# The hand-written order of weight splits against attention steps in the mixing layers of a two-block network, moved by a tile or a unit

## The reference

```python
def second_block(x, ...):
    for i in range(2):
        x = x + 0.5 * _swiglu(_rmsnorm(x, ffn1_norm[i]), ...)      # 1024 -> 2 x 2816 -> 1024
        x = x + _mixing(_rmsnorm(x, mix_norm[i]), ...)             # the layer that is changed
        x = x + 0.5 * _swiglu(_rmsnorm(x, ffn2_norm[i]), ...)
    return _rmsnorm(x, final_norm)
```

## Time and profile before

| What | Value |
|---|---|
| Median of 3 runs (lowest, highest) | 1243.99 us (1242.6, 1244.24) |
| Profiled execution: its time, its span | 1242.6 us, 1240.8 us |
| Mean granted TensorE clock | 0.997 |
| Busy in the span: PE, DVE, ACT, POOL | 99%, 70%, 55%, 13% |
| TensorE's weight loads busy | 94% |
| HBM read, mean rate | 218.48 MB, 177 GB/s |

### The profile page before, as it was taken

The page is one execution under the profiler, slowest core; times in us unless marked ns, Lnnn a source line. Parts: engine busy times, 40 slices in busy tenths (PEclk is TensorE's granted clock), DMA queues, the critical chain, the costliest instruction groups (busy, mean ns, idle before and its releaser), DMA issues.

```text
span 1240.8 us, 24135 instructions
## 1 busy us (share of the span) xinstructions
PE 1229.7 (99%) x10072; PEld 1160.3 (94%) x10072; DVE 869.3 (70%) x1372; ACT 684.7 (55%) x1100; POOL 160.2 (13%) x210
## 2 busy tenths in 40 slices
PE   9999999999999999999999999999999999999997
PEld 7889878999999988899999999999998889999997
DVE  6988798878665557867666556677556777766742
ACT  7674666555545466556554544555447566555541
POOL 4201500275000110012000010000120002000001
PEclk9999999999999999999999999999999999999998
DMA  9545643556565554345555555655555444655550
GB/s 328 183 120 176 240 138 127 178 181 211 191 200 187 188 185 138 119 137 193 199 190 201 188 187 204 201 185 186 194 186 171 137 134 139 204 203 183 191 188 35
DMA packets 61388, 221.09 MB, mean 178 GB/s; under 512 B 7264, under 2 KB 7392, under 8 KB 61024
## 3 DMA queue, kind: packets, MB, share of 16 engines
q1 hardware_dynamic: 60768, 218.87, 53.4%
q0 software_dynamic: 224, 0.53, 0.2%
q10 hardware_dynamic: 288, 0.16, 0.0%
HBM read 218.48 MB, written 1.05 MB: 177 GB/s over the span
## 4 chain that ended last, share of the span: by engine, by line
PE 94%; DVE 4%; ACT 1%; issue 1%; POOL 1%; DMA 0%; POOLq 0%; ACTq 0%; DVEq 0%
PE pb L476 13%; PE pb L478 13%; PE pb L477 13%; PE pb L491 8%; PE pb L493 8%; PE pb L492 8%; PE pb L456 7%; PE pb L458 7%; PE pb L457 7%; PE pb L549 3%; DVE s_acc L1388 2%; PE pb L578 1%; DVE s_wl L1236 1%; PE pb L602 1%; PE pb L736 1%
## 5 line engine op out<-in xcount | busy, mean ns | idle before, releaser
L1236 DVE TENSOR_TENSOR s_wl<-s_wraw,s_wh 128x1024 fp32r<-128x1024 f32 (+1 forms) x411 | 501.7, 1241 | 125.9 <-ACT s_wh L877 125.4
L877 ACT ACTIVATE s_wh<-s_wraw 128x1024 fp32r<-128x1024 f32 (+1 forms) x411 | 420.8, 1048 | 181.1 <-PE pb L478 83.0
L476 PE MATMUL pb<-s_xh,s_wh 128*128 128x256 f32 x1296 | 359.1, 277 | 0.0
L478 PE MATMUL pb<-s_xh,s_wl 128*128 128x256 f32 x1296 | 358.3, 276 | 0.0
L477 PE MATMUL pb<-s_xl,s_wh 128*128 128x256 f32 x1296 | 358.3, 276 | 0.0
L477 PEld LDWEIGHTS pb<-s_xl,s_wh 128*128 128x128 f32 x1296 | 243.5, 188 | 0.0
L476 PEld LDWEIGHTS pb<-s_xh,s_wh 128*128 128x128 f32 x1296 | 243.5, 188 | 0.0
L478 PEld LDWEIGHTS pb<-s_xh,s_wl 128*128 128x128 f32 x1296 | 243.4, 188 | 0.0
L456 PE MATMUL pb<-s_wh,s_xh 128*128 128x512 f32 x448 | 180.9, 404 | 1.6 <-DVE s_wl L1236 1.6
L491 PE MATMUL pb<-s_hh,s_wh 128*128 128x256 f32 x660 | 182.2, 276 | 0.0
L492 PE MATMUL pb<-s_hl,s_wh 128*128 128x256 f32 x660 | 182.2, 276 | 0.0
(11 more groups left out here) (313 smaller groups left out, 1590.7 us busy)
## 6 DMA issues: line engine op xcount, KB each, us to landing
s_wraw<-in_w SPq DMA_DIRECT2D x407, 512.0 KB, 4.1
s_nab<-in_rpb SPq DMA_DIRECT2D x2, 1024.0 KB, 9.4
s_x<-in_x SPq DMA_DIRECT2D x4, 256.0 KB, 5.4
out_dram<-s_at_s SPq DMA_DIRECT2D x4, 256.0 KB, 2.6
s_cst<-in_cst SPq DMA_DIRECT2D x1, 680.0 KB, 9.1
s_wraw<-in_w SPq DMA_DIRECT2D x2, 256.0 KB, 4.6
s_ln<-in_lng POOLq DMA_DIRECT2D x2, 128.0 KB, 7.5
s_ln<-in_lnb POOLq DMA_DIRECT2D x2, 128.0 KB, 8.3
```

What stands on the lines that cost most here:

```text
L476: pe.matmul(o, wh[:, s, w], xk[0], start=k == v == 0, stop=False, skip_group_check=True)
L478: r = pe.matmul(o, wl[:, s, w], xk[0], start=False, stop=k == 7, skip_group_check=True)
L877: return act.activation(o, src, ACT.Copy, scale=scale)
L1236: dve.tensor_tensor(wl[:, s, part], wraw[:, r, part], wh[:, s, part].bitcast(F32), ALU.subtract).then_inc(low_done, 1)
```

## The change

Nothing is added and nothing is taken away: the same instructions stand in another order, on TensorE, ScalarE and VectorE, in `mixers2`, which both mixing phases execute.

- TensorE: the transposes "lq" and "lk" with level 4, the scores of L0 with level 5, and the transposes of L0 with the scores of L1 and level 6 stand one tile later each. The transposes of L1 stay after tile 54.
- ScalarE: unit 28 is copied ahead of the exponential of L0 and no longer behind the sigmoid.
- VectorE: unit 24 is split ahead of the copy of transposed F1 (before: behind `blocks(2)`); unit 25 ahead of `turn_dilated` (before: behind `blocks(3)`); unit 27 ahead of the copy of "lk" (before: behind `blocks(4)`, and units 25 and 26 stood here); unit 28 ahead of `low_dil(0)`; units 29 and 30 ahead of the copy of transposed L0 (before: 28 and 29); unit 31 ahead of `normalise(n, "L", 1)` (before: 30 and 31 stood behind it).

```diff
             level(3)
-            tiles(n, 44)
+            tiles(n, 45)
             pe.wait_ge(turned_done, 4 * l + 4)
...
             level(4)
-            tiles(n, 47)
+            tiles(n, 48)
...
             level(5)
-            tiles(n, 50)
+            tiles(n, 51)
             turn_weights(n, "L", 0)
...
             copy(flat(fqt[:, 0:2, :]), psum(n, "lq")[:, :]).then_inc(*empty(n, "lq"))
-            split(n, 28)
+            split(n, 29)
             exponential(n, "L", 0)
...
             normalise(n, "F", 1)
+            split(n, 25)
             turned_weights("F", 1, None)
             advance(2)
             blocks(2)
-            split(n, 25)
+            split(n, 26)
             dve.wait_ge(turn_sin, 2)
             dve.wait_ge(dia_done, 8 * (l + 1))
             turn_dilated(0)
...
             blocks(3)
-            split(n, 27)
+            split(n, 28)
             dve.wait_ge(*full(n, "lk"))
...
             blocks(4)
-            split(n, 28)
+            split(n, 29)
             low_dil(0)
             advance(5)
             blocks(5)
             normalise(n, "L", 0)
-            split(n, 30)
+            split(n, 31)
             turned_weights("L", 0, "yF")
             low_dil(1)
             advance(6)
             blocks(6)
+            split(n, 32)
             normalise(n, "L", 1)
-            split(n, 32)
             turned_weights("L", 1, "yF")
```

## The result

The changed kernel takes 1252.26 us (median of 4 runs, 1251.99 to 1252.55) against 1244.12 us (1242.6 to 1244.73): 8.1 us slower, ratio 1.0067, 95% interval 1.0050 to 1.0085. Forecast were 1249.7 us and a range up to 1252.0. The profiled execution is not among the four; it took 1250.78 us with a span of 1249.0; against the span of before (1240.8) that is 8.2 us more, so the trace can be read for the whole difference.

A forecast was written before the change was run, and what follows sets the result against it. TensorE, busy 55.00 of 55.00 us in the changed stage, was taken as the bound. Per layer 2.47 + 1.55 - 1.23 + 0.05 = 2.84 us of waiting, 5.7 us in all: 1243.99 + 5.7 = 1249.7 us, range 1246.6 to 1252.0.

The forecast's parts named there:

- what bounds the kernel: Changed stage: TensorE is busy 55.00 of 55.00 us, so the change can gain next to nothing and can only lose.
- TensorE's moves: Mixing stage: the same matmuls in another order cost or give nothing by themselves; moved steps come 1.37 us later.
- the wait for unit 25: VectorE ahead of turn_dilated: a wait of 4.6 us for ScalarE's copy, which doesn't reach TensorE.
- The slack at "lq" and at level 4: TensorE's "lq" transposes and level 4: VectorE's results come 1.4 and 0.7 us before they are needed, so no wait.
- the sum of the waits: TensorE at the transposes of L1: 2.84 us of waiting in a layer, 5.7 us in both.
- 2.47: VectorE at low_dil(0): starts 2.47 us later, 1.37 from TensorE's tile and 1.10 from the splits.
- 1.55: VectorE ahead of the normalising of L1: unit 31 costs 1.55 us, 0.41 idle and 1.14 of work.
- 1.23: Before the transposes of L1: the old order had 1.23 us of slack (done 526.95, needed 528.18), subtracted from the loss.
- 0.05: At the transposes of L1: 0.05 us from VectorE's end to TensorE's start, added in each layer.
- The first delay: TensorE at the transposes of L0: a likely wait of 0.3 us, not added to the sum.
- The clock falls in the wait: Rival, chance 0.06: TensorE's clock drops to 1.2 GHz for 5 us behind each wait, 5 us more, 1254.7 us.
- high bound of the waits: Both mixing layers: 2 x (2.97 + 1.55 - 1.23 + 0.35) = 7.3 us, with slower subtractions and the L0 wait counted.

The follow-up runs named there:

- mended form: Changed kernel with unit 31 split behind the normalising of L1 again and TensorE's transposes of L1 one tile later: 1243.49 us, ratio 0.9996.
- unit 31 back: Changed kernel with VectorE's subtraction of unit 31 behind the normalising of L1 again, as before the change: 1246.47 us, ratio 1.0020.
- unit 28 back: Changed kernel with VectorE's split of unit 28 behind the normalising of L0, ScalarE keeping its new order: 1247.19 us, ratio 1.0024.
- clock held up: Changed kernel with 11 added identity matmuls in front of TensorE's wait for the normalised L1: 1249.36 us, ratio 1.0043.
- second comparison: Changed kernel measured once more, unedited, beside the kernel before in the last set: 1250.46 us, ratio 1.0054.
- unit 25 back: Changed kernel with VectorE's split of unit 25 behind blocks(3) again, so the rotation doesn't wait for ScalarE: 1250.20 us, ratio 1.0055.
- four delays: Kernel before with four added VectorE instructions, some 1.2 us each, ahead of the normalising of L1 in each mixing layer: 1255.15 us, ratio 1.0090.

## Why the prediction was wrong, point by point

**Right: what bounds the kernel.** TensorE had no wait to lose in the stage, so nothing was gained, by the change or by its mended form (1243.49 against 1243.78).

**Right: TensorE's moves cost next to nothing by themselves**, shown by running them alone (0.2 us a layer in the trace). The slack that they take away costs 0.7 us a layer once the splits are moved too.

**Right: the wait for unit 25 is absorbed**, shown by taking it out: the start of `low_dil(0)` keeps its distance, 7.83 us. The slack at "lq" and at level 4 held, no wait stands there; with TensorE's tile taken back, level 4 waits 0.64 us.

**Right: the sum of the waits.** 2.47 + 1.55 - 1.23 + 0.05 = 2.84 us a layer; 2.82 and 2.77 were measured. Its parts were shown one by one by the delays in the traces: with unit 31 back 1.56 of 2.82 go (1.55 in the sum), with unit 28 back 1.05 (1.10 in the sum), and with TensorE's moves undone 0.7. The first delay, 0.3 us at the transposes of L0, was 0.24 and hidden, as the sum had it. With the clock held up, the kernel takes 1249.36 us, where the forecast has 1249.7.

**Wrong: "The clock falls in the wait".** The prediction had this as a rival with a chance of 0.06, "possible, not likely", and left it out of the sum. This is the step that failed. The argument against it was that the wait of 1.6 us at the start left the clock at 1.00. Between this row and a wait of 2.4 us of idleness nothing was known, and such a gap is no reason for 0.06. The runs showed in its place: 0.83, 1.03, 1.06 and 1.59 us of idleness in front of the transposes left the clock alone (eight of eight layers), 2.3 to 2.4 us let it fall in six of eight, 3.58 us in two of two. The one row that I leaned on was also of another kind than the wait it stood for: it lies at the start, 0.7 us behind the moment at which the clock had risen. The price that the rival gave, 2.5 us a layer, was too high for this wait: 1.48 and 1.67 us were lost. The stretch at the lower clock is some three microseconds, and the prediction took five; behind the longer wait of 3.58 us one layer did lose 2.75.

**The range.** Its upper end, 1252.0, came from a high bound of the waits (7.3 us would make 1251.3; the other 0.7 has no term) and left the clock out by choice. With the two waits and the measured price of the clock the sum is 1244.0 + 5.7 + 3.2 = 1252.9, of which the small gains elsewhere take half a microsecond. The second comparison of the same kernel, 1250.46, lies inside. One kernel thus has medians 1.8 us apart, at waits of 2.39 us each time; that the clock behind equal waits can differ is shown within one execution of the kernel with unit 25 back; the mean clocks on record point the same way, but that this is the whole of the 1.8 us is argued, not shown.

**Open.** What decides, at 2.3 to 2.4 us of idleness, whether the clock falls was not tried. It isn't the loads beside it: it fell with none running. Nor does the fall keep a distance to the wait: in the changed kernel TensorE stops at 529.28 and the clock falls at 531.26, before the wait ends (0.88 as the mean of 530.00 to 531.66); in its second profiled execution TensorE stops at 528.67, starts again at 531.06, and the clock falls only at 532.1 (0.56 as the mean of 532 to 533). Nor is the length of one wait the whole condition: near the end of the kernel before, where TensorE is busy 1.15 of 2 us, the clock fell at a wait of 1.0 us. The cause of the 0.3 us between the values and the last transposes stays open as well. The change is not what gives them: they show in five of the eight layers in which the clock fell behind a wait of 2.3 us or more (one with unit 25 back and one with four delays among them), not in the other three, and in no layer in which it stayed. So a part of what the clock takes is given back behind the values.

## What to carry to other kernels

Where a saturated TensorE is fed by in-order engines, the price of a reordering is worked out along the chain of the feeding engine, piece by piece from the timeline, up to each moment at which TensorE needs something; here that gave every start of VectorE's to 0.05 us and the two waits to 0.07. A wait that is new on TensorE must then be priced twice, by its length and by the clock behind it: if the trace of before has no idle time of that length in a busy stretch, the lower clock is a case with a real chance and not a remote one. And a step that is moved closer to what it waits for has to keep its slack: one unit's split put behind the normalising and one tile more ahead of the transposes, together, were the difference between 8 us and nothing.

## What the runs showed of the hardware

- A wait of 2.3 to 2.4 us of TensorE in a stage that was busy before lowers the granted clock from 1.00 to 0.50 in some executions and layers, with a loss of 1.5 to 1.75 us behind it (six of eight layers); 0.83 to 1.6 us did in none of eight, 3.58 us did in both layers, with losses of 2.75 and 1.71 us. At the start of the kernel, where the clock has only just risen, the clock was up behind 1.1 to 1.8 us (ten executions) and down behind 2.0 us (three), but there the wait is longer when the clock rose earlier. The Trainium skill (TensorE: Matmul & The Clock Gate, HAM oscillation) has the mechanism: idle time between bursts of matmuls brings the clock to half, and the next burst starts at half speed. The traces agree, but for two of the falls (the second layer with unit 25 back, the first of the changed kernel's second execution), which came only after TensorE had started again. The idle gap that its rule still allows is longer than the 2.3 to 2.4 us that sufficed here, and the measurement decides.
- The granted clock of the profile can miss a stretch at the lower level: it says 1.00 for 7 to 10 us in the kernel with four delays, while matmuls of 512 columns start 0.43 us apart, against 0.23 at full speed.
- Matmuls that nobody needs, issued into a bank that is overwritten next, hold the clock: with 11 of them in the wait the kernel is 5.6 us slower than before, against 8.1 and 6.9 us for the changed kernel in its two comparisons.
- A float32 matmul of 128 x 128 by 128 columns is recorded twice and took 0.223 us, while transposes of the same shape took 0.11 us.
